# Stick-breaking heads: the strict mask set by GpSimd on the sigmoids instead of added by TensorE to the logits

## The reference, cut to what matters

```
z = (q @ k.T) * scale                       # 512 x 512 for each head
strict = kpos[None, :] < qpos[:, None]      # key strictly before the query
log_beta = log_sigmoid(z)
log_keep = where(strict, log_sigmoid(-z), 0.0)
between  = reverse_cumsum(log_keep) - log_keep
w   = where(strict, exp(log_beta + between), 0.0)
out = w @ v
```

## Time and profile before

| | |
|---|---|
| median of 3 runs | 1943.32 us (1941.65 to 1943.45) |
| the profiled execution | 1941.8 us |
| its span in the trace | 1940.1 us |
| busy: PE, PEld, DVE, ACT, POOL | 1911.5, 1600.5, 979.8, 809.0, 303.6 us |
| granted TensorE clock, mean | 0.999 of full speed |

### The profile page before, as it was taken

One profiled execution on the slowest core, in us unless ns is written; L12 is line 12 of the kernel. 1 busy time (PEld: TensorE's weight loads), 2 busy tenths in 40 slices (PEclk: granted clock), 3 DMA queues, 4 the chain that ended last, 5 costly groups with the idle time before them and its releaser, 6 DMA issues.

```text
span 1940.1 us, 24515 instructions
## 1 busy us (share of the span) xinstructions
PE 1911.5 (99%) x9718; PEld 1600.5 (82%) x9718; DVE 979.8 (51%) x1541; ACT 809.0 (42%) x1424; POOL 303.6 (16%) x378
## 2 busy tenths in 40 slices
PE   9999999999999999999999999999999999999998
PEld 7888778988888888878898888888878788888887
DVE  5566777522233357589842233336668962223334
ACT  4445866422222234367533232223547743323222
POOL 2133344000000010003412220001002312221000
PEclk9999999999999999999999999999999999999999
DMA  7212111233333222221133333332121224333331
GB/s 239 57 55 93 55 44 40 81 109 98 98 98 93 96 75 75 88 88 44 55 120 98 96 90 97 98 98 85 59 87 44 67 76 121 97 97 98 98 98 55
DMA packets 97138, 167.78 MB, mean 86 GB/s; under 512 B 8160, under 2 KB 49152, under 8 KB 97024
## 3 DMA queue, kind: packets, MB, share of 16 engines
q1 hardware_dynamic: 97024, 166.21, 28.0%
HBM read 164.09 MB, written 2.10 MB: 86 GB/s over the span
## 4 chain that ended last, share of the span: by engine, by line
PE 87%; ACT 5%; DVE 5%; POOL 2%; issue 2%; DMA 0%; SPq 0%; DVEq 0%; POOLq 0%; ACTq 0%
PE ps L49 83%; PE ps L52 3%; DVE wlo L71 1%; POOL p L71 1%; ACT sk1h L65 1%; ACT p L62 1%; ACT whi L65 1%; ACT L62 1%; DVE p L91 1%; POOL hTl L71 1%; DMA raw<-in_w_in_dram 0%; DVE pS L91 0%; DVE rot L71 0%; DVE x L71 0%; DVE hTl L71 0%
## 5 line engine op out<-in xcount | busy, mean ns | idle before, releaser
L65 ACT ACTIVATE whi<-raw 128x1024 fp32r<-128x1024 f32 (+1 forms) x294 | 310.1, 1055 | 728.8 <-PE ps L49 725.7
L71 DVE TENSOR_TENSOR wlo<-raw,whi 128x1024 fp32r<-128x1024 f32 (+1 forms) x294 | 361.2, 1229 | 394.9 <-ACT whi L65 392.0
L49 PE MATMUL ps<-hTh,whi 128*128 128x512 f32 (+1 forms) x1176 | 442.3, 376 | 0.0
L49 PE MATMUL ps<-hTh,wlo 128*128 128x512 f32 (+1 forms) x1176 | 437.7, 372 | 0.0
L49 PE MATMUL ps<-hTl,whi 128*128 128x512 f32 (+1 forms) x1176 | 437.6, 372 | 0.0
L49 PE MATMUL ps<-whi,uh 128*128 128x512 f32 x688 | 268.0, 390 | 0.0
L49 PE MATMUL ps<-whi,ul 128*128 128x512 f32 x688 | 267.7, 389 | 0.0
L49 PE MATMUL ps<-wlo,uh 128*128 128x512 f32 x688 | 267.7, 389 | 0.0
L49 PEld LDWEIGHTS ps<-hTh,wlo 128*128 128x128 f32 x1176 | 220.8, 188 | 39.5
L49 PEld LDWEIGHTS ps<-hTh,whi 128*128 128x128 f32 x1176 | 221.0, 188 | 36.9 <-DVE wlo L71 0.4
L49 PEld LDWEIGHTS ps<-hTl,whi 128*128 128x128 f32 x1176 | 221.1, 188 | 36.5
(11 more groups left out here) (241 smaller groups left out, 2300.2 us busy)
## 6 DMA issues: line engine op xcount, KB each, us to landing
raw<-in_w_ff_dram SPq DMA_DIRECT2D x128, 512.0 KB, 3.6
raw<-in_w_gate_up_dram SPq DMA_DIRECT2D x88, 256.0 KB, 3.1
raw<-in_w_in_dram SPq DMA_DIRECT2D x40, 512.0 KB, 4.6
raw<-in_w_in_dram SPq DMA_DIRECT2D x68, 256.0 KB, 3.1
raw<-in_w_down_dram SPq DMA_DIRECT2D x22, 512.0 KB, 3.5
raw<-in_w_o_dram SPq DMA_DIRECT2D x16, 512.0 KB, 4.1
x<-in_x_dram SPq DMA_DIRECT2D x8, 512.0 KB, 6.5
raw<-in_w_out_dram SPq DMA_DIRECT2D x8, 512.0 KB, 3.8
```

The source lines that it names most:

```text
L49: return self.eng.matmul(out, l, r, start=start, stop=stop, skip_group_check=True)
L65: return self.eng.activation(out, in_, ACT.Copy)
L71: return self.eng.tensor_tensor(out, a, b, op)
```

## The change

The mask product and the tile `m_strict` go away, and the first product with the keys opens the bank. The logits of the query's own key and of later keys are then left as they are. A new POOL step `lsx` (`late_mask`) follows the first sigmoid: it sets `lk` to 1 from the query's own key on, by an affine select on the last 128 keys of each part. DVE's scan waits for `lsx` instead of `lsc`. After its product, POOL waits for its own result (`lsm`), and a second select sets the product to 0 in the same places. The transposes wait for that one. The planner gets the new step and new durations, and so it makes a new order for all queues in both layers.

```diff
-                P.add(("llg", k), "PE", 0.12 + sum(2 * max(0.109, N / 2260 + 0.007) for _, _, N in part), ...
+                P.add(("llg", k), "PE", 0.02 + sum(2 * max(0.109, N / 2260 + 0.007) for _, _, N in part), ...
-                P.add(("lsn", k), "DVE", sum(0.12 + 0.00215 * N for _, _, N in part), ("lsc", k), seq="lw", pri=2)
-                P.add(("lsw", k), "POOL", 0.25 + 0.00164 * w, ("lsn", k), ("lsk", k), seq="lm", pri=2)
+                P.add(("lsx", k), "POOL", 0.2 + 0.0012 * 128 * len(part), ("lsc", k), seq="lx", pri=1)
+                P.add(("lsn", k), "DVE", sum(0.12 + 0.00215 * N for _, _, N in part), ("lsx", k), seq="lw", pri=2)
+                P.add(("lsw", k), "POOL", 0.5 + 0.00164 * w + 0.0012 * 128 * len(part), ("lsn", k), ("lsk", k), seq="lm", pri=2)
...
-                    if len(part) == 2:
-                        pe.mm(ps[b][:, :].rearrange("p (a n) -> p a n", a=2)[:, :, 0:128], identB[:, :], bc(m_strict[:, :], 1, [128, 2, 128]), True, False)
-                    else:
-                        N = part[0][2]
-                        pe.mm(ps[b][:, N - 128:N], identB[:, :], m_strict[:, :], True, False)
...
-                        pe.mm(ps[b][:, c0:c0 + N], q, kh[:, 0:N], False, False)
+                        pe.mm(ps[b][:, c0:c0 + N], q, kh[:, 0:N], j == 0, False)
...
-                    dve.wait_ge(*at("lsc", k))
+                    dve.wait_ge(*at("lsx", k))
...
-            for mk in (m_causal, m_strict, m_chunk):
+            for mk in (m_causal, m_chunk):
...
-            pool.select(m_strict[:, :], m_strict[:, :], [[-1, 128]], -1, 1, NEG)
...
+        def own_keys(ap, part, fillv):
+            if len(part) == 2:
+                v = ap[:, :].rearrange("p (a n) -> p a n", a=2)[:, :, 0:128]
+                return pool.select(v, v, [[0, 2], [-1, 128]], -1, 1, fillv)
+            N = part[0][2]
+            return pool.select(ap[:, N - 128:N], ap[:, N - 128:N], [[-1, 128]], -1, 1, fillv)
+
+        def late_mask(m):
+            for it in STICK:
+                for r_, part in enumerate(it["banks"]):
+                    k = (m, "S", it["i"], r_)
+                    yield T["lsx", k]
+                    pool.wait_ge(*at("lsc", k))
+                    own_keys(buf(("lk", m, it["i"], r_), p2[1]), part, 1.0).then_inc(*up("lsx", k))
...
-                    pool.tt(bt[:, 0:w - 1], bt[:, 0:w - 1], kp[:, 1:w], ALU.mult).then_inc(*up("lsw", k))
+                    pool.tt(bt[:, 0:w - 1], bt[:, 0:w - 1], kp[:, 1:w], ALU.mult).then_inc(*up("lsm", k))
+                    pool.wait_ge(*at("lsm", k))
+                    own_keys(bt, part, 0.0).then_inc(*up("lsw", k))
...
-            parts += [norm("a%d" % m), key_zeros(m), late_fin(m), late_weight(m), ...
+            parts += [norm("a%d" % m), key_zeros(m), late_fin(m), late_mask(m), late_weight(m), ...
```

More of the change, by code:

```diff
@@ L229, in decoder_program @@
     m_causal = r.t("m_causal", [128, 128], BF16)
-    m_strict = r.t("m_strict", [128, 128], BF16)
     m_chunk = r.t("m_chunk", [128, 128], BF16)
@@ L789, in plan_late @@
                 k, w = (m, "S", i, r_), width(it, part)
-                P.add(("llg", k), "PE", 0.12 + sum(2 * max(0.109, N / 2260 + 0.007) for _, _, N in part), *[("evV", (m, "S%d" % it["half"], j)) for j in range(4)],
+                P.add(("llg", k), "PE", 0.02 + sum(2 * max(0.109, N / 2260 + 0.007) for _, _, N in part), *[("evV", (m, "S%d" % it["half"], j)) for j in range(4)],
                       kept[-4] if len(kept) >= 4 else None, seq="llg", pri=3, take=[("T", [("lsk", k)])])
@@ L2727, in pool_program @@
         for m in (1, 2):
-            parts += [norm("a%d" % m), key_zeros(m), late_fin(m), late_weight(m), mix_straight(m), norm("f%d" % m), up_evac(m)]
+            parts += [norm("a%d" % m), key_zeros(m), late_fin(m), late_mask(m), late_weight(m), mix_straight(m), norm("f%d" % m), up_evac(m)]
         parts.append(norm("z"))
```

## The result

The changed kernel takes **1962.62 us** (median of 4 runs, 1961.88 to 1963.36), the kernel before 1942.62 us beside it (1941.65 to 1943.45). The ratio is 1.0105, 95% interval 1.0093 to 1.0117: slower by 1%, 20 us, where I forecast 3. The time lies 9 us above the upper end of my range. Single executions of one kernel fall in two groups some 1.4 us apart (before: near 1941.8 and near 1943.2), so differences of 1 to 2 us between two medians are read only with their intervals. The profiled execution takes 1961.9 us, its span is 1960.1.

What follows compares the result with a forecast made beforehand. PE, busy 99% of the span, was taken as the bound, full only because filler and chain end together. Per layer -1.5 + 2.34 + 0.65 gave +1.5, both +3.0: 1943.3 + 3.0 = 1946.3 us, range 1937.9 to 1953.5.

Steps and rivals of the forecast that it cites:

- the sum: Per layer: masks -1.5, three passages +2.34, port +0.65, making +1.5; both layers +3.0 us.
- The three later passages: Later part of each stretch, chain from scan over POOL's product to transposes: three passages lengthened 0.78 us each, +2.34 a layer.
- two hand-overs: Passage from logits to transposes: two hand-overs at 0.10 us each, beside two selects of 0.29, making 0.78.
- The selects' own durations: On POOL: 0.29 us for one part, 0.40 for two; 15.7 us a layer.
- The masks' price: On PE: 0.12 us a mask (bounds 0.11 and 0.14), 6.0 us in both layers; half credited, -1.5 a layer.
- The port: DVE's scan and POOL's selects contend: 0.13 us a bank, five banks' scans, +0.65 us a layer.
- The new order: Planner's new order in all queues: priced by no row, some 2 us either way.
- the third: Rival: DVE is held at each scan by POOL's queue and port lock, 7.8 us in both layers, 1951.1 us; chance 27%.
- The first: Rival: PE stays fed, chunks cover the longer passage and PE sheds 6.0 us, 1937.3 us; chance 18%.
- the second rival: The two cancel: filler covers one passage of three, no select meets a scan, within 1 us of 1943.3; chance 13%.
- My mark for the forecast itself: PE's idle time in each stretch rises from 3.4 to about 8 us; the forecast itself had 42%.

Runs made afterwards that it cites:

- e2: Kernel before with the mask products left out and nothing put in their place, old order of all queues: 1939.9 us, ratio 0.9988.
- e4: Changed kernel's new order in all queues, but neither select issued and no masking in the heads: 1947.7 us, ratio 1.0027.
- e3: The change with both selects, but planner durations and steps as before, so queues keep the old order: 1962.7 us, ratio 1.0108.
- e12: Kernel before without mask products or selects, mask carried in DVE's scan, narrow product, factor of key j kept in column j, old order: 1939.7 us, ratio 0.9990.
- e1: Changed kernel with the 48 mask products put back on PE, both selects and new order kept: 1962.4 us, ratio 1.0105.
- e7: As e3, old order without mask products, but each select replaced by two fills of idle tiles that read nothing: 1960.6 us, ratio 1.0095.
- e5: Kernel before, mask products and old order kept, with only the first select added, between sigmoid and scan: 1950.6 us, ratio 1.0043.
- e6: Kernel before, mask products and old order kept, with only the second select added, between product and transposes: 1951.7 us, ratio 1.0046.
- e9: Kernel before without mask products or selects, mask in DVE's scan, narrow POOL product, factor of key j + 1 in column j, old order: 1943.6 us, ratio 1.0009.

## Why the prediction was wrong, point by point

**The step that failed is the sum**: "The three later passages pay 3 x 0.78 = +2.34". I charged the selects with 4.7 us in both layers, and 1.3 for the port. They measure 22.8 us in the old order and 14.9 in the new one; the order, which stood outside the sum, adds 7.8 there. The stretch from 868 us to the transposes of the next norm, layer 1, by the same windows in each kernel:

| kernel | length | PE busy | PE idle | clock |
|---|---|---|---|---|
| before | 95.05 | 91.62 | 3.43 | 1.00 |
| e2, no masks | 94.30 | 89.97 | 4.33 | 1.00 |
| e4, new order, no selects | 98.00 | 90.69 | 7.31 | 0.98 |
| e3, selects, old order | 103.50 | 91.56 | 11.94 | 1.00 |
| after | 104.35 | 93.25 | 11.10 | 0.97 |
| e12, mask in the scan | 94.00 | 89.78 | 4.22 | 1.00 |

From e2 to e3 the idle time rises by 7.6 us in this layer alone, with no new order and at full clock. Two things were wrong in the term. A passage is not lengthened by the selects' durations and two hand-overs (0.78), but by what POOL and DVE have queued ahead: up to 1.9 us at one scan. And not three passages pay, but most: DVE stands 13 times in layer 1 for a first select in e3 (11.4 us; 6 times and 4.0 us in the changed kernel), and even an early bank is not covered: at 883.78 us of e3 PE waits 1.75 for a second select. I had written down what is queued behind the waits, and did not price it. That these had only some tenths to spare I read from the earlier trace rows, which show how busy the engines are, and not what waits.

**The selects' own durations** were right: 0.29 us for one part, and 0.41 for two, where I took 0.40. There are 96. But beside DVE single ones become up to 1.2 us, and POOL is busy 58 us in the stretch, not 53.

**The masks' price** was nearly right, and their worth too high. 0.12 a mask is 0.10 over the 21 banks without waits, below the 0.11 that I had named as the least, so by that mark too the prediction was wrong. Three banks a layer gave time back as waits. I credited 3.0 us; e2 gives 2.0, and in the changed kernel they are worth nothing (e1). The doubt that I put in the bound ("none, if the chain leads everywhere") was the case in the changed kernel. That filler covers the first half of the stretch, the ground for crediting half of the masks, did not hold either: from 868 to 921 us PE waits 3.8 us for POOL's selects in e3 and 1.9 in the changed kernel.

**The port** (1.3 us) measures 2.1 in e7, with an interval from none to 7: not contradicted, and no more than that.

**The new order** was "some 2 us either way", and stood outside the sum. It is +7.8 without the selects. With them it neither helps nor hurts: e3 and the changed kernel take the same.

**The clock** was not in the forecast. After PE's gaps the granted clock falls, in layer 1 to 0.74 in one window of 10 us. Summed over windows of 20 us in both stretches, what is missing to full clock is 7.0 us of time in the changed kernel and 3.6 in e3, which takes as long. So it can be up to 7 of the 20 us. The selects' cost does not need it: in layer 1 e3 loses 8.45 us against before at full clock. In the changed kernel it is a part: from e4 to it, with the same products in the same order, PE's busy time in layer 1 rises from 90.69 to 93.25 us. No run here holds the clock fixed, so its own share stays open.

**The rivals.** By the test that I gave, the third (DVE held at each scan) is the one that came true: DVE waits for POOL before scans for 4.0 us a layer, over the 3 that I named. Its mechanism is half of what the experiments show: e5 has it alone and costs 8.8 us. The other half, PE held by POOL's second select before the transposes, costs 9.9 in e6, where DVE waits for no select. Its price, 0.49 us a bank and "some half" of it given back by DVE's idle time, made 7.8 us of what was 20. The first and the second rival needed PE to stay fed, in all or in part, which 11.10 us of idle time rule out. My mark for the forecast itself, PE's idle time at about 8 us, was met to the letter (8.39 from 868 to 968), and was worth little: the stretch no longer ended at 963 but at 972.35. A mark must be tied to a piece of work, not to a window of time.

## What to carry to other kernels

Where three in-order queues hand small steps to one another and the fourth engine has just enough filler, an instruction put into such a hand-over can cost its place in the queue more than its duration: here 24 banks a layer and two selects each, some 32 us of instructions (undisturbed, both layers) on an engine that idles most of the time, made 22.8 us, while the same select placed early cost a third of what it cost late. Count for each such step how late it runs behind what is queued ahead, and who is queued behind the engine that it holds; move what can go early out of the chain (9.9 us became 3.2), or better, fold it in an instruction that is there already (the scan's second operation: nothing measurable). Price a new order by itself, too (e4: 7.8 us). And take an engine's price for freed work only where that engine leads.

## What the runs showed of the hardware that I had not expected

The duration of a product of two SBUF operands on POOL depends on where the second one begins: in place with the second operand at column 1, 383 columns take 0.86 us and 511 take 1.09; with both at column 0 1.00 and 1.28 (e9 against e12, which differ in nothing else on POOL). No run moves the first operand, so whether it is the offset between the two or the place of the second alone stays open. In this chain that was 3.9 us of the kernel's time (1943.6 against 1939.7).

The granted clock of PE fell after gaps of 2.48 and 0.81 us, on PE's timeline of the changed kernel:

```profile
951.54 0.63 PE L49 MATMUL ps<-whi,hTh 128*128 128x512 f32 x1
951.97 0.63 PE L49 MATMUL ps<-wlo,hTh 128*128 128x512 f32 x1
```

Their starts lie 0.43 us apart, where the same products lie 0.23 apart at 942 us: the lower of the two levels, 1.2 GHz. They lie 0.43 apart in e4 as well, from 945.22 on, after its gap of 2.45 us. e3 idles as long in the same stretch, but in pieces of at most 1.8 us, and its clock stays at 1.00 there; in layer 2 it too falls, to 0.93 and 0.91 in two windows of 20 us. What decides it I can't say from these runs.
